# Gates folded into the output weights of a second feed-forward stage, with the residual accumulated in place

## The reference

```
def swiglu(h, w_up, w_down):
    a, u = jnp.split(h @ w_up, 2, axis=-1)
    return (jax.nn.silu(a) * u) @ w_down
...
    x = layer_norm(ALPHA * x + 0.5 * g1 * swiglu(x * (1.0 + sc1) + sh1, w_f1_in, w_f1_out), ln_g[0], ln_b[0])
    y, aux = mixer(x * (1.0 + sc2) + sh2)
    x = layer_norm(ALPHA * x + g2 * y, ln_g[1], ln_b[1])
    x = layer_norm(ALPHA * x + 0.5 * g3 * swiglu(x * (1.0 + sc3) + sh3, w_f2_in, w_f2_out), ln_g[2], ln_b[2])
```

## Time and profile before

| | |
|---|---|
| median of 3 runs | 2934.59 us (2934.52 to 2943.79) |
| profiled execution | 2934.64 us |
| its span, first to last instruction | 2932.9 us |
| mean granted PE clock, share of full | 0.938 |
| PE busy | 2615.3 us, 89% |
| DVE busy | 1908.1 us, 65% |
| ACT busy | 803.7 us, 27% |
| POOL busy | 237.7 us, 8% |
| second feed-forward stage | about 2077 to 2932.9 us |

### The profile page before, as it was taken

One profiled execution on the slowest core, in us unless ns is written; L12 is line 12 of the kernel. 1 busy time (PEld: TensorE's weight loads), 2 busy tenths in 40 slices (PEclk: granted clock), 3 DMA queues, 4 the chain that ended last, 5 costly groups with the idle time before them and its releaser, 6 DMA issues. The chain is left out here.

```text
span 2932.9 us, 37788 instructions
## 1 busy us (share of the span) xinstructions
PE 2615.3 (89%) x15240; PEld 1630.3 (56%) x15240; DVE 1908.1 (65%) x2825; ACT 803.7 (27%) x1204; POOL 237.7 (8%) x226
## 2 busy tenths in 40 slices
PE   6899999999997758887799999657699999999985
PEld 6555555555554646766566676523355555555542
DVE  2577777777677767776456565588365555555578
ACT  0511111111213436666333233120412111111111
POOL 0000000000000211110201011002030000000064
PEclk9999999999998989999899999779699999999997
DMA  6323232322121010000111000032241111111001
GB/s 227 105 79 101 88 100 91 97 72 87 44 73 56 39 42 1 1 1 1 44 32 39 14 5 4 15 124 94 72 149 45 43 48 52 43 43 43 29 1 65
DMA packets 150267, 169.23 MB, mean 58 GB/s; under 512 B 8264, under 2 KB 125284, under 8 KB 149107
## 3 DMA queue, kind: packets, MB, share of 16 engines
q1 hardware_dynamic: 150130, 167.33, 17.7%
HBM read 152.46 MB, written 14.84 MB: 57 GB/s over the span
## 5 line engine op out<-in xcount | busy, mean ns | idle before, releaser
L1175 PE MATMUL psum<-act_hi,ffn_win_hi 128*128 128x384 f16 x2112 | 691.4, 327 | 8.2 <-DVE ffn_win_lo L1444 8.2
L1175 PE MATMUL psum<-act_lo,ffn_win_hi 128*128 128x384 f16 x2112 | 691.3, 327 | 0.0
L1175 PE MATMUL psum<-act_hi,ffn_win_lo 128*128 128x384 f16 x2112 | 691.1, 327 | 0.0
L1343 ACT ACTIVATE ffn_silu<-psum,ffn_win_inverse 128x384 f32<-128x384 f32 x132 | 76.6, 580 | 1104.0 <-PE psum L1175 1102.0
L1206 PE MATMUL psum<-ffn_wout_hi,ffn_h_hi 128*128 128x512 f16 x792 | 309.8, 391 | 31.2 <-DVE ffn_gated L1006 15.5
L1502 DVE SCALAR_TENSOR_TENSOR Y<-psum,ffn_h_unit,Y 128x512 f32<-128x512 f32 x324 | 239.8, 749 | 110.6 <-PE psum L1206 108.6
L1206 PE MATMUL psum<-ffn_wout_lo,ffn_h_hi 128*128 128x512 f16 x792 | 309.5, 391 | 0.0
L1206 PE MATMUL psum<-ffn_wout_hi,ffn_h_lo 128*128 128x512 f16 x792 | 308.9, 390 | 0.0
L1175 PEld LDWEIGHTS psum<-act_hi,ffn_win_hi 128*128 128x128 f16 x2112 | 207.6, 98 | 145.0 <-DVE ffn_win_lo L1444 8.5
L1175 PEld LDWEIGHTS psum<-act_hi,ffn_win_lo 128*128 128x128 f16 x2112 | 207.4, 98 | 138.0 <-issue 2.2
L1175 PEld LDWEIGHTS psum<-act_lo,ffn_win_hi 128*128 128x128 f16 x2112 | 207.4, 98 | 137.0 <-issue 2.3
(11 more groups left out here) (325 smaller groups left out, 4463.7 us busy)
## 6 DMA issues: line engine op xcount, KB each, us to landing
ffn_win_raw<-in_w_in SPq DMA_DIRECT2D x88, 512.0 KB, 5.1
w_mod<-in_w_mod SPq DMA_DIRECT2D x36, 1024.0 KB, 5.0
ffn_wout_raw<-in_w_out SPq DMA_DIRECT2D x44, 512.0 KB, 4.3
scan_w_raw<-in_w_mix SPq DMA_DIRECT2D x20, 512.0 KB, 5.2
x_after<-Y SPq DMA_DIRECT2D x9, 512.0 KB, 2.6
mixout_residual<-x_after SPq DMA_DIRECT2D x9, 512.0 KB, 3.4
x_after<-mixout_x_row SPq DMA_DIRECT2D x9, 512.0 KB, 2.7
ffn_residual<-x_after SPq DMA_DIRECT2D x9, 512.0 KB, 12.0
```

The costliest lines, as they stand in the source:

```text
L1175: last = nc.tensor.matmul(bank[:, 0:CH], win[b][w][:, half, k, :], K.A[a][:, k, c * CH:(c + 1) * CH], start=(n == 0), stop=(n == 3 * KT - 1))
L1343: nc.scalar.activation(sa[s][:], pa[s][:, 0:CH], ACT.Silu, scale=winv[:, b:b + 1]).then_inc(silu, 1)
```

## The change

Only the second feed-forward stage computes in another way:

- `wout_scale` multiplies each of the two weight rows with both gates (latent and context), 2 x 1024 values into `gated`, and takes the maximum over these. The high and the low parts are made of them, twice as wide; PE reads the second set for the context tile. The gates are thus in the product already.
- Y starts as the residual, scaled by ALPHA: the mixing output stage now scales its LayerNorm rows (`gB`, `bB`) by ALPHA before it makes the x rows that it stores, and SP loads these straight into Y, ahead of the opening group. All groups add onto Y. In the last group `tile` adds the scaled PSUM halves onto Y and takes the statistics at once.
- POOL keeps only the reciprocal root. ACT no longer scales rows. DVE ends every row by `finish_row`, one tile later (the last one at once).
- The gates are loaded before SP's first wait, and DVE waits for them before the opening group and for the residual before the next.

```diff
 
     def start(self, dve):
         self.link = Chain(dve, self.chain)
-        if self.before is not None:
-            dve.wait_ge(self.gates, 64)
-            for rows in (self.gR, self.bR):
-                self.link(self.nc.vector.tensor_scalar(rows[:], rows[:], ALPHA, None, ALU.mult))
+        dve.wait_ge(self.gates, 64)
+        dve.wait_ge(self.rows, 32)
+        for rows in (self.gR[:], self.bR[:], self.gB, self.bB):
+            self.link(self.nc.vector.tensor_scalar(rows, rows, ALPHA, None, ALU.mult))
...
+        self.gate = place(f"{tag}_gate_rows", [P, 2, D])
+        self.gated = place(f"{tag}_wout_gated", [P, GB, 2, D])
-        self.part = [place(f"{tag}_gated_{i}", [P, D]) for i in range(2)]
...
+    def load_gates(self, sp):
+
+        for v in range(2):
+            sp.dma_start(self.gate[:, v, :], self.K.mod_rows[v:v + 1, self.gate_i * D:(self.gate_i + 1) * D]
+                         .broadcast_to([P, D])).then_inc(self.gates, 16)
+
+    def load_residual(self, sp):
+
+        for t in range(NT):
+            sp.dma_start(self.K.Y[:, t, :], self.res_src(t)).then_inc(self.res, 16)
+
+    def load_rows(self, sp):
...
-        for v in range(2):
-            sp.dma_start(self.gate[:, v, :], K.mod_rows[v:v + 1, self.gate_i * D:(self.gate_i + 1) * D]
-                         .broadcast_to([P, D])).then_inc(self.rows, 16)
...
         for t in range(NT):
-            sp.dma_start(self.res[:, t, :], self.res_src(t)).then_inc(self.rows, 16)
-
-    def store(self, sp):
-
-        for t in range(NT):
-            if t < NT - 1:
-                sp.wait_ge(self.row_done, t + 1)
-            else:
-                sp.wait_ge(self.last_done, 1)
+            sp.wait_ge(self.row_done, t + 1)
             sp.dma_start(self.out_dst(t), self.K.Y[:, t, :]).then_inc(self.stored, 16)
...
-        gp.wait_ge(self.rows, 16 * (NT + 4))
         for t in range(NT):
-            link(nc.gpsimd.tensor_scalar(self.res[:, t, :], self.res[:, t, :], ALPHA, None, ALU.mult))
-        def bracket(t):
-            gp.wait_ge(y_added, summed_before + 2 * t + 2)
-            link(nc.gpsimd.tensor_tensor(Y[:, t, :], Y[:, t, :], self.gate[:, int(t == CTX_T), :], ALU.mult))
-            nc.gpsimd.tensor_tensor(Y[:, t, :], Y[:, t, :], self.res[:, t, :], ALU.add).then_inc(self.bracketed, 1)
...
-        def shift(t):
-            gp.wait_ge(self.unit, t + 1)
-            nc.gpsimd.tensor_tensor(Y[:, t, :], Y[:, t, :], self.bB[:], ALU.add).then_inc(self.row_done, 1)
-
-        for t in range(NT):
-            bracket(t)
-        for t in range(NT):
-            root(t)
-            if t:
-                shift(t - 1)
...
         for half in range(2):
             m, cols = 2 * t + half, slice(half * 512, (half + 1) * 512)
             dve.wait_ge(y_ready, done + m + 1)
-            nc.vector.scalar_tensor_tensor(part[:, cols], py[m % 3], self.q[:, c:c + 1], self.gate[:, int(t == CTX_T), cols],
-                                           ALU.mult, ALU.mult).then_inc(y_added, 1)
-        dve.wait_ge(y_added, done + 2 * t + 5)
-        dve.wait_ge(self.bracketed, t + 1)
-        nc.vector.tensor_tensor(Y[:, t, :], Y[:, t, :], part[:], ALU.add).then_inc(self.summed, 1)
-        dve.wait_ge(self.summed, t + 1)
+            nc.vector.scalar_tensor_tensor(Y[:, t, cols], py[m % 3], self.q[:, c:c + 1], Y[:, t, cols],
+                                           ALU.mult, ALU.add).then_inc(y_added, 1)
-        for h in range(2):
-            link(nc.vector.bn_stats(self.st[:, h, :], Y[:, t, h * 512:(h + 1) * 512]))
+        for half in range(2):
+            dve.wait_ge(y_added, done + 2 * t + half + 4)
+            link(nc.vector.bn_stats(self.st[:, half, :], Y[:, t, half * 512:(half + 1) * 512]))
...
-    def unit_rows(self, act, t):
-
-        act.wait_ge(self.centred, t + 1)
-        act.wait_ge(self.rstd, t + 1)
-        self.nc.scalar.activation(self.K.Y[:, t, :], self.K.Y[:, t, :], ACT.Copy, scale=self.rs[:, t:t + 1]).then_inc(self.unit, 1)
-
-    def last_row(self, dve):
-
-        t, Y = NT - 1, self.K.Y
-        dve.wait_ge(self.centred, NT)
-        dve.wait_ge(self.rstd, NT)
-        self.nc.vector.scalar_tensor_tensor(Y[:, t, :], Y[:, t, :], self.rs[:, t:t + 1], self.bB[:], ALU.mult, ALU.add).then_inc(self.last_done, 1)
+    def finish_row(self, dve, t):
+
+        Y = self.K.Y
+        dve.wait_ge(self.centred, t + 1)
+        dve.wait_ge(self.rstd, t + 1)
+        self.nc.vector.scalar_tensor_tensor(Y[:, t, :], Y[:, t, :], self.rs[:, t:t + 1], self.bB[:], ALU.mult, ALU.add).then_inc(self.row_done, 1)
...
+        GV = 1 if first else 2
+        wout = [place(f"{tag}_wout_{x}", [P, GB, GV, D], F16) for x in ("hi", "lo")]
...
+            if end:
+                end.load_gates(sp)
...
+                end.load_residual(sp)
                 group(0)
-                end.load(sp)
+                end.load_rows(sp)
...
-                                                    wout[w][:, b, half * 512:(half + 1) * 512],
+                                                    wout[w][:, b, 0 if mod else int(t == CTX_T), half * 512:(half + 1) * 512],
...
-                    nc.scalar.activation(wout[0][:, b, :], oraw[b][:], ACT.Copy, scale=os_[:, b:b + 1]).then_inc(out_hi, 1)
+                    nc.scalar.activation(wout[0][:, b], oraw[b][:].unsqueeze(1) if mod else end.gated[:, b], ACT.Copy,
+                                         scale=os_[:, b:b + 1]).then_inc(out_hi, 1)
...
-                end.unit_rows(act, 0)
                 gate(i, 0, 2, n=4)
-                end.unit_rows(act, 1)
-                end.unit_rows(act, 2)
                 gate(i, 1, 2, n=5)
                 chunk_hi(2)
-                for t in range(3, NT - 1):
-                    end.unit_rows(act, t)
...
-                    link(largest(nc, omax[:, b:b + 1], oraw[b][:]))
+                    if mod:
+                        link(largest(nc, omax[:, b:b + 1], oraw[b][:]))
+                    else:
+                        link(nc.vector.tensor_tensor(end.gated[:, b], oraw[b][:].unsqueeze(1).broadcast_to([P, 2, D]), end.gate[:], ALU.mult))
+                        link(largest(nc, omax[:, b:b + 1], end.gated[:, b].rearrange("p v n -> p (v n)")))
...
-                    nc.vector.scalar_tensor_tensor(wout[1][:, b, :], oraw[b][:], os_[:, b:b + 1], wout[0][:, b, :],
-                                                   ALU.mult, ALU.subtract).then_inc(out_lo, 1)
+                    nc.vector.scalar_tensor_tensor(wout[1][:, b], oraw[b][:].unsqueeze(1) if mod else end.gated[:, b], os_[:, b:b + 1],
+                                                   wout[0][:, b], ALU.mult, ALU.subtract).then_inc(out_lo, 1)
...
                 chunk_scale(1)
                 chunk_lo(i, 1)
                 tile(1)
+                end.finish_row(dve, 0)
                 tile(2)
+                end.finish_row(dve, 1)
                 product(i, 0, 0, 2, n=4)
                 tile(3)
+                end.finish_row(dve, 2)
                 product(i, 0, 1, 2, n=5)
                 chunk_max(2)
                 chunk_scale(2)
                 chunk_lo(i, 2)
                 for t in range(4, NT):
                     tile(t)
-                end.last_row(dve)
+                    end.finish_row(dve, t - 1)
+                end.finish_row(dve, NT - 1)
...
+                dve.wait_ge(end.gates, 32)
                 group(0, 0, 0, first=True)
                 link.at = link.n
-                per = 24
+                per = 26
                 link.begin(1, per, link.at - per)
-                group(1, 1, 1, fresh=True)
+                dve.wait_ge(end.res, 16 * NT)
+                group(1, 1, 1)
```

22 lines of the change are left out of this document (9 added, 13 removed).

## The result

The changed kernel takes 2918.95 us, the median of five runs (2918.28 to 2922.60), against 2934.59 us before (here the median of five runs too, 2933.66 to 2943.79): 15.6 us less, ratio 0.9946 with a 95% interval of 0.9934 to 0.9958. The profiled execution of the changed kernel took 2918.28 us, its span 2916.4 us, 16.5 us shorter than the span before.

What follows compares the result with a forecast made beforehand. TensorE matmuls bound the loop, VectorE the last 43 us. Terms: last group -4.6, tail -8.3, opening group +3.7, sum -9.2 us from 2934.64: 2925.4 us; range 2919.5 to 2931.

Steps and rivals of the forecast that it cites:

- opening group, pause: Opening group: PE stands still 2.0 us for the product behind the longer wout_scale, and nothing absorbs it.
- opening group, clock: Opening group: eight matmuls at half clock behind PE's pause, charged 1.7 us; the ends are 0 and 2.3 us.
- last group, path to the first down matmul: Last group up to its middle: low parts and both parts of h done at 2847.4 instead of 2849.46, gain 2.05 us.
- from there to the second chunk, addition and clock: Last group's down-projection: 1.24 us for the dropped addition, plus clock; with the path 3.3 to 5.9 us, middle 4.6 taken.
- tail: Last 44.6 us, DVE's own: four tiles 6.1, filled root wait 0.8, last row 2.0, later root -0.6; gain 8.3 us.
- Rival (3): Tail: POOL's root operations hold up DVE's two-input operations 1.5 us in five tiles, +7.5: 2932.9 us; chance 0.06.
- Rival (4): Loop: cover breaks if multiplications exceed 3.4 us each; at 4.6 us every group stalls, 2967 us; chance 0.05.
- Rival (2): Ahead of the opening group: opening transfers come late, up to 3 us: 2928.4 us; chance 0.07.
- (a): Opening group: half clock behind the 2.0 us pause, charged 1.7 us from a 2.18 us pause in the first feed-forward stage.
- (b): Last group's first down tiles: 5.2 us at half clock, 2.6 at full; the middle was taken.
- (c): Last group, up to the third chunk's scale at 2888.35: PE runs nearly without a gap, so the shift arrives unchanged.
- first rival: Opening pause and first down tiles: full clock at both, -12.2 us, 2922.4 us; chance 0.25.

Runs made afterwards that it cites:

- opening_filled: opening_moved with 52 idle matmuls in TensorE's 3.23 us pause behind the last group's first chunk; 2916.46 us, ratio 0.9941.
- pauses_filled: Kernel before, with idle matmuls (160 and 70) in TensorE's last-group pauses of 9.76 and 4.62 us; 2931.25 us, ratio 0.9991.
- rows_by_dve: Kernel before, with each row ended by one VectorE operation instead of ScalarE scaling and GpSimd shift; 2931.55 us, ratio 0.9996.
- rows_by_pool: Changed kernel, with rows 0 to 7 again ended by ScalarE and GpSimd, row 8 by VectorE; 2916.18 us, ratio 0.9939.
- row_meets_centring: rows_by_pool with GpSimd's row moved ahead of its root operations, so it stands beside VectorE's centring; 2923.86 us, ratio 0.9959.
- opening_moved: Changed kernel, with the product TensorE waits for moved ahead of the second gated multiplication in the opening group; 2918.52 us, ratio 0.9946.
- last_gate_first: Changed kernel, with ScalarE's silu ahead of the weights' high parts in the last group; 2919.66 us, ratio 0.9953.
- combined: Changed kernel with the edits of opening_moved, last_gate_first and rows_mixed together; 2911.86 us, ratio 0.9918.
- rows_mixed: Changed kernel, with rows 0 to 6 ended by ScalarE and GpSimd, rows 7 and 8 by VectorE; 2915.72 us, ratio 0.9934.
- opening_long: Changed kernel, with the opening group's second gated multiplication done three times; 2924.18 us, ratio 0.9961.
- opening_longer: Changed kernel, with the opening group's second gated multiplication done twice; 2925.08 us, ratio 0.9969.
- combined_filled: combined with 66 and 52 idle matmuls in TensorE's pauses ahead of the last down-projection and behind its first chunk; 2908.76 us, ratio 0.9912.

## Why the forecast missed

Step by step, measured against forecast, in the us of the two profiled executions:

| step | forecast | measured | what showed it |
|---|---|---|---|
| loop groups | 0 | 0 | no PE pause; multiplication 2.28 us |
| opening transfers, mixing stage | 0 | 0 | VectorE's idle time: 1.30 us in place of 2.78 ahead of the mixing stage's first tile, 5.80 in place of 5.73 ahead of the opening group's maximum |
| opening group, pause | +2.0 | +2.0 | changed kernel, opening_filled |
| opening group, clock | +1.7 | 0 | full clock in five traces |
| last group, path to the first down matmul | -2.05 | -2.1 | table: 755.02 less 2.03, against 755.09 |
| from there to the second chunk, addition and clock | -2.55 | -3.8 | changed kernel; pauses_filled for the clock |
| second to third chunk | 0 | -2.3 | pauses_filled, 1.8 and a wait of 0.5 |
| tail | -8.3 | -9.7 | rows_by_dve, rows_by_pool |
| ahead of the stage | 0 | -0.6 | starts differ by up to 2.8 us between the kernels |
| sum | -9.2 | -16.5 | |

**Right: the mechanism and the path lengths up to the down-projection.** Cover in the loop, the 2 us pause, the 2.05 us at the down-projection, and where the tail gains, if not how much. The forecast calls 62 us a loop group, and a group is 70.98 us; nothing in the sum hangs on it, since the cover was worked out from the places of the operations. Rival (3) fell: beside the root operations VectorE's row end takes 1.28 us, and it is GpSimd's that waits (1.46 in place of 0.57 us), as the forecast had charged with 0.6. Rival (4), broken cover, fell with the 2.28 us. Rival (2) fell: VectorE's maximum behind the opening load starts 5.74 us behind the stage's first matmul, 5.67 before.

**Wrong: TensorE's clock, in three terms of the sum, 5.3 of the 7.3 us between 9.2 and 16.5.** (a) The half clock behind the opening pause was taken from one row of another stage, whose pause was longer by 0.14 us only; the choice between 0 and 2.3 us went the wrong way, by 1.7. Why the one pause has half clock behind it and the other not is open. (b) The first down tiles were put halfway between half and full clock, when the terms were at hand: I had worked out that VectorE would be done 2 us earlier and that TensorE would stand still for 5 us, which is in the middle of a block that it still had to compute. So the long pause lay ahead of the block's last 24 matmuls, of which the half-clock ones (15 of 0.53 us behind the row at 2841.23) are covered by VectorE's low parts, and the down-projection itself had a pause of 0.58 us. The full-clock end was the one to take: 1.3 us. (c) "From there PE runs nearly without a gap, so it arrives unchanged at the third chunk's scale" was not so: ahead of it lay a pause of 4.62 us with half clock behind it, in the trace of before and in none of the rows above. Timeline of PE, before:

```profile
2863.47 0.61 PE L1206 MATMUL psum<-ffn_wout_hi,ffn_h_hi 128*128 128x512 f16 x1 [4.62 <-DVE ffn_gated L1006]
2863.87 0.63 PE L1206 MATMUL psum<-ffn_wout_lo,ffn_h_hi 128*128 128x512 f16 x1
```

It shrank to 3.23 us and the clock stayed full: 2.3 us, of which pauses_filled gives back 1.8 and VectorE's late maximum holds the rest. The forecast's first rival had (a) and (b), at 2922.4 us; (c) and the tail's 1.4 us below were in no case, which is why the range ended too high. The last 0.6 us, ahead of the stage, is scatter of the stage's start and no gain of the change.

**Wrong by size: the tail, 1.4 us.** The four tiles gave 1.73 us each in place of 1.52. I had summed durations, and on VectorE back-to-back operations start closer than their durations say: a row's end of 1.28 us costs 1.20 us from start to start, and the addition of 2.77 us cost 2.80 (0.08 us a tile). The other 0.13 us a tile is a wait: the addition needed both halves of the tile, the first of the statistics now needs only the first half, so from the pair's start to what follows 1.31 us pass in place of 1.44. Four tiles make 0.85 us; the rest is 0.15 us in the first tile and 0.4 us behind the last centring.

**Stays open.** Nine traces have the pause of 3.23 us behind the first chunk. In three of them (changed, rows_by_pool, row_meets_centring) the clock stays full, in three (opening_moved, last_gate_first, combined) it is half at once, and in three (rows_mixed, opening_long, opening_longer) it falls some matmuls later; the stretch then takes 1.3 to 2.8 us more. I don't know what puts a kernel in which group: its length is the same, and rows_by_pool and rows_mixed differ in nothing that has run by then but in their place in time. The Trainium skill, page "TensorE: Matmul & The Clock Gate", section "Part 1: The HAM clock gate", says that the window in which the chip watches TensorE's activity runs free of the kernel's start, so that the point at which the clock changes varies. By that the same pause could come out either way; the nine traces fit, and no run here moved that phase by itself. Part of the changed kernel's gain, the 2.3 us of (c), may then be something its executions don't all have: its five runs reach from 2918.28 to 2922.60 us, and the profiled one is the fastest.

## What to carry to other kernels

When work is moved off the end of a kernel, list TensorE's pauses in the stretch with the clock behind each, and forecast a time for every one at half and at full clock: here the path to the down-projection came out within 0.1 us and the clock made 5 of the 7 us missed. Then ask which block stands behind the longest pause, the one on the path or one that other work covers. A GpSimd row cost VectorE nothing here beside operations that read PSUM or one operand from SBUF, and its whole remaining length, less 0.1 to 0.2 us, beside one with two SBUF operands, so place it rather than remove it. And sum start-to-start distances, not durations.

## What was not expected of the hardware

- The same pause of 3.23 us at the same instruction has full clock behind it in one kernel and half in another, with the nearest edit 700 us earlier (opening_moved) or none that has run by then (rows_mixed against rows_by_pool): 1.7 us lost without any change near, for a reason that stays open.
- Idle matmuls can be worth their place: 118 of them took the median of the three edits together from 2911.86 to 2908.76 us (combined_filled), 230 took 4.2 us off the stage of the kernel before.
- VectorE's two-input operation ended 1.07 to 1.09 us behind GpSimd's row in eleven places where they met, whatever the overlap: 2.77 us long in place of 1.22 for the addition, 3.47 and 3.28 us in place of 1.28 for the others.
